# A hybrid block and two attention layers on one core: the first norm's sums folded on VectorE, the identity loaded by itself, modulation copies and one branch's masks put earlier

## What is computed

```python
def rmsnorm(x, g):
    y = xf * lax.rsqrt(jnp.mean(xf * xf, axis=-1, keepdims=True) + EPS)
    return (y * g).astype(x.dtype)

h = rmsnorm(x, norm1_g[l])                       # first norm
(hg_q, hg_f, hg_i, hg_g, ml_qk, ...) = jnp.split(h @ w_in[l], split_at, axis=-1)
# third branch, ssd_scan, per chunk (all chunks are taken as one here):
L = jnp.exp(jnp.where(tri, cum[..., :, None] - cum[..., None, :], NEG_BIG))
CB = jnp.repeat(jnp.einsum('btgn,bsgn->bgts', Cc, Bc), hpg, axis=1)
y_intra = jnp.einsum('bhts,bshp->bthp', CB * L, xdt)
# second block, per layer:
sh1, sc1, g1, sh2, sc2, g2 = modulation(c, w_ada[i], b_ada[i])
```

## Time and profile before

| | us |
|---|---|
| three runs | 1884.54, 1893.31, 1894.9 |
| their median | 1893.31 |
| the profiled execution, and its span | 1895.75, 1894.0 |
| PE busy | 1803.6 (95%) |
| DVE, ACT, POOL busy | 1014.4, 872.5, 358.4 |
| mean granted clock of PE | 0.962 of full speed |

### The profile page before, as it was taken

How to read it: one execution, slowest core, us unless ns; L and a number is a source line. 1 busy time by engine, 2 the same in 40 slices (tenths; PEclk the granted TensorE clock), 3 DMA queues, 4 the chain that set the end, 5 groups by cost and what they waited for, 6 DMA issues and landing times.

```text
span 1894.0 us, 30494 instructions
## 1 busy us (share of the span) xinstructions
PE 1803.6 (95%) x12882; PEld 1619.9 (86%) x12882; DVE 1014.4 (54%) x1760; ACT 872.5 (46%) x1261; POOL 358.4 (19%) x220
## 2 busy tenths in 40 slices
PE   7999989999999999999998999999999897889999
PEld 6999888888999999998866778877888786689999
DVE  1376469676766882465544165413552366438750
ACT  4422545547445664444653144312433345546653
POOL 4402540000000116500001301142114100041137
PEclk9999989999999999999986989999999898979999
DMA  6554445455455544511100332254223221025544
GB/s 253 208 193 167 168 189 189 156 201 200 193 221 212 190 167 138 178 68 46 46 1 1 134 112 89 75 188 171 98 83 121 95 90 67 1 90 180 183 151 155
DMA packets 40823, 258.78 MB, mean 137 GB/s; under 512 B 4336, under 2 KB 7408, under 8 KB 14320
## 3 DMA queue, kind: packets, MB, share of 16 engines
q1 hardware_dynamic: 40688, 256.84, 37.1%
HBM read 255.77 MB, written 1.05 MB: 136 GB/s over the span
## 4 chain that ended last, share of the span: by engine, by line
PE 83%; DVE 11%; ACT 3%; issue 1%; DMA 1%; POOL 1%; SPq 0%; DVEq 0%; ACTq 0%
PE acc_psum L194 22%; PE acc_psum L195 21%; PE acc_psum L196 21%; PE acc_psum L2213 4%; PE acc_psum L2173 2%; PE acc_psum L235 2%; DVE w_low_sb L160 2%; PE acc_psum L2195 2%; PE acc_psum L319 2%; PE acc_psum L911 2%; PE acc_psum L254 1%; DMA con_sb<-in_con 1%; DVE norm_sq_sb L570 1%; DVE norm_rt_sb L1561 1%; POOL w_low_sb L160 1%
## 5 line engine op out<-in xcount | busy, mean ns | idle before, releaser
L194 PE MATMUL acc_psum<-h_high_sb,w_high_sb 128*128 128x256 f32 (+1 forms) x2144 | 667.5, 311 | 9.1 <-DVE h_low_sb L379 4.4
L196 PE MATMUL acc_psum<-h_high_sb,w_low_sb 128*128 128x256 f32 (+1 forms) x2144 | 658.8, 307 | 0.0
L195 PE MATMUL acc_psum<-h_low_sb,w_high_sb 128*128 128x256 f32 (+1 forms) x2144 | 658.6, 307 | 0.0
L149 ACT ACTIVATE w_high_sb<-ring_sb 128x1024 fp32r<-128x1024 f32 (+2 forms) x412 | 386.6, 987 | 455.3 <-PE acc_psum L196 250.4
L194 PEld LDWEIGHTS acc_psum<-h_high_sb,w_high_sb 128*128 128x128 f32 x2144 | 411.8, 192 | 40.0 <-issue 16.8
L160 POOL TENSOR_TENSOR w_low_sb<-ring_sb,w_high_sb 128x1024 fp32r<-128x1024 f32 (+2 forms) x150 | 297.3, 2005 | 744.2 <-ACT w_high_sb L149 744.2
L195 PEld LDWEIGHTS acc_psum<-h_low_sb,w_high_sb 128*128 128x128 f32 x2144 | 411.5, 192 | 19.2 <-issue 0.5
L196 PEld LDWEIGHTS acc_psum<-h_high_sb,w_low_sb 128*128 128x128 f32 x2144 | 410.9, 192 | 18.4
L160 DVE TENSOR_TENSOR w_low_sb<-ring_sb,w_high_sb 128x1024 fp32r<-128x1024 f32 (+1 forms) x262 | 306.6, 1211 | 85.7 <-ACT w_high_sb L149 75.9
L1774 DVE SCALAR_TENSOR_TENSOR u_filtered<-acc_psum,par_sb,u_filtered 128x255 f32<-128x255 f32 (+2 forms) x264 | 150.8, 571 | 151.4 <-ACT u_filtered L1881 139.2
L1909 POOL TENSOR_TENSOR u_low<-u_filtered,u_high 128x256 fp32r<-128x256 f32 (+1 forms) x66 | 61.0, 924 | 785.0 <-ACT u_high L1902 785.0
(11 more groups left out here) (290 smaller groups left out, 2143.0 us busy)
## 6 DMA issues: line engine op xcount, KB each, us to landing
ring_sb<-in_w_in SPq DMA_DIRECT2D x68, 1024.0 KB, 6.4
ring_sb<-in_w_up SPq DMA_DIRECT2D x66, 1024.0 KB, 4.8
ring_sb<-in_w_ada SPq DMA_DIRECT2D x48, 1024.0 KB, 4.9
ring_sb<-in_w_down SPq DMA_DIRECT2D x48, 704.0 KB, 4.1
ring_sb<-in_w_out SPq DMA_DIRECT2D x12, 1024.0 KB, 5.1
ring_sb<-in_w_br_hg SPq DMA_DIRECT2D x4, 1024.0 KB, 7.4
ring_sb<-in_w_br_ml SPq DMA_DIRECT2D x4, 1024.0 KB, 7.8
ring_sb<-in_w_br_mb SPq DMA_DIRECT2D x4, 1024.0 KB, 8.4
```

Of the source, the lines that this page charges most:

```text
L149: self.nc.scalar.activation(self.high[:, g % 2, piece], self.ring[:, c % RING, piece], ACT.Copy)\
L194: nc.tensor.matmul(out, sh, mh, start=start, stop=False)
L195: nc.tensor.matmul(out, sh, ml, start=False, stop=False)
L196: return nc.tensor.matmul(out, sl, mh, start=False, stop=stop)
```

## The change

- The identity is loaded by a DMA of its own, right behind x; the later DMA of the constants takes the rest (`con[:, P:]`). PE waits for the identity alone ahead of the spread, and for the rest at unit 1.
- ACT first takes a Sqrt of two constants (into `norm1.tokens`, overwritten later), then squares, then makes the first unit's high part, then the root. Before, the high part stood behind the root.
- DVE adds the four tiles of squares in three operations of 512 columns and one of 256; PE sums the one folded tile with `folded_sums`, two products in place of 16.
- DVE waits for `par` behind the reciprocal, no longer ahead of it.
- In DVE's loop the modulation copy stands right behind the read-out of unit n - 1, ahead of the scan steps of the first branch and of the low part of unit n + 1.
- In iteration 45 `mb_keep_cb` stands ahead of the reciprocal and values of the second branch's norm.

```diff
--- before.py
+++ after.py
@@ -321,6 +321,15 @@
                                                stop=(k == len(self.streams) - 1 and t == DT - 1 and b == ST - 1), skip_group_check=True)
         if p == DT // 2 - 1:
             mm.then_inc(*self.summed.one())
+
+    def folded_sums(self, pe, folded):
+
+        core = self.core
+        pe.wait_ge(*folded.at(1))
+        for b in range(ST):
+            mm = core.nc.tensor.matmul(core.psum[:, self.bank, b:b + 1], self.streams[0].v(0)[:, b * P:(b + 1) * P], core.ones[:, 0:1],
+                                       start=(b == 0), stop=(b == ST - 1), skip_group_check=True)
+        mm.then_inc(*self.summed.one())
 
     def root(self, act, *biases):
 
@@ -710,6 +719,8 @@
                 for half in range(2):
                     sp.dma_start(X[:, 4 * half:4 * half + 4, 0:S], a["x"].rearrange("(k p) t -> p k t", p=P)[:, 4 * half:4 * half + 4, :])\
                         .then_inc(*x_ready[half].dma())
+                o_, w_ = CON_AT["ident"]
+                sp.dma_start(con[:, o_:o_ + w_], a["con"][:, o_:o_ + w_]).then_inc(*sig("identity_ready").dma())
                 core.load(sp, 0)
                 sp.dma_start(par[:, :], a["par"]).then_inc(*par_ready.dma())
 
@@ -841,6 +852,7 @@
         "parameters_ready", "constants_set", "constants_ready", "conditions_ready"))
     done, act_read, dve_read = sig("unit_done"), sig("unit_read_by_act"), sig("unit_read_by_dve")
     filtered, conv_read = sig("conv_filtered"), sig("conv_read")
+    folded, identity = sig("squares_folded"), sig("identity_ready")
     mk_ready, wg_ready, mk_kept = sig("level_masks_ready"), sig("gate_weights_ready"), sig("level_masks_kept")
     mixed_ready, mixed_high, mixed_low = sig("mixed_ready"), sig("mixed_high_ready"), sig("mixed_low_ready")
 
@@ -1272,7 +1284,7 @@
         def _(sp):
             for c in range(1, RING):
                 core.load(sp, c)
-            sp.dma_start(con[:, :], a["con"]).then_inc(*con_ready.dma())
+            sp.dma_start(con[:, P:], a["con"][:, P:]).then_inc(*con_ready.dma())
             sp.dma_start(lv_in, a["levels"]).then_inc(*mk_ready.dma())
             sp.dma_start(flat(wg), a["w_gates"]).then_inc(*wg_ready.dma())
             core.release(sp, UNITS, mods[0])
@@ -1340,12 +1352,14 @@
                     mods[r // NM].reduce(pe, r, r % NM)
 
             pe.wait_ge(*const_set.at(1))
-            for p in range(DT // 2):
-                norm1.sums(pe, p)
-
-            pe.wait_ge(con_ready.handle, 16)
+            norm1.folded_sums(pe, folded)
+
+            pe.wait_ge(identity.handle, 16)
             norm1.spread(pe)
             for n in range(UNITS):
+                if n == 1:
+
+                    pe.wait_ge(con_ready.handle, 16)
                 unit(n)
                 modulation(n)
                 for i in hg_steps(n):
@@ -1453,15 +1467,15 @@
                 s = 2 * (c % 2)
                 nc.scalar.activation(dst, conv_tmp[:, s:s + 2, :], ACT.Silu).then_inc(*conv_read.one())
 
+            act.wait_ge(*const_set.at(1))
+            nc.scalar.activation(norm1.tokens, core.eps[:, 0:2], ACT.Sqrt)
             for p in range(DT // 2):
                 if p % 2 == 0:
 
                     act.wait_ge(x_ready[p // 2].handle, 16)
                 norm1.square(act, p)
-
-            act.wait_ge(*const_set.at(1))
+            core.split_high(act, 0)
             norm1.root(act, core.eps[:, 0:1])
-            core.split_high(act, 0)
             norm1.highs(act)
 
             act.wait_ge(par_ready.handle, 16)
@@ -1594,8 +1608,16 @@
                 if b == 2:
                     dve.sem_inc(*mixed_ready.one())
 
+            sq = core.norm_sq
+            dve.wait_ge(*norm1.at(norm1.squared, 2))
+            link(nc.vector.tensor_tensor(sq[:, 0, :], sq[:, 0, :], sq[:, 1, :], ALU.add))
+            dve.wait_ge(*norm1.at(norm1.squared, 4))
+            link(nc.vector.tensor_tensor(sq[:, 2, :], sq[:, 2, :], sq[:, 3, :], ALU.add))
+            link(nc.vector.tensor_tensor(sq[:, 0, :], sq[:, 0, :], sq[:, 2, :], ALU.add))
+            nc.vector.tensor_tensor(sq[:, 0, 0:S], sq[:, 0, 0:S], sq[:, 0, S:2 * S], ALU.add).then_inc(*folded.one())
+            norm1.reciprocal(dve)
+
             dve.wait_ge(par_ready.handle, 16)
-            norm1.reciprocal(dve)
             norm1.parts(dve)
             for n in range(UNITS + 1):
                 if n == 1:
@@ -1604,6 +1626,9 @@
                     nc.vector.tensor_reduce(mods[0].select, cn("ident").rearrange("p (g s) -> p s g", g=4)[:, 0:2, :], AX.X, ALU.add)
                 if n >= 1:
                     evict(n - 1)
+                if n - 1 in rides:
+                    r = rides.index(n - 1)
+                    mods[r // NM].copy(dve, r)
                 steps = list(hg_steps(n - 1))
                 for i in steps[:1]:
                     hg_step(dve, i)
@@ -1611,9 +1636,6 @@
                     low(n + 1)
                 for i in steps[1:]:
                     hg_step(dve, i)
-                if n - 1 in rides:
-                    r = rides.index(n - 1)
-                    mods[r // NM].copy(dve, r)
                 if n == 2 * NM + 1:
                     mods[0].read(dve, NM, 0, NM).then_inc(*first_read.one())
                 if n == 4:
@@ -1638,6 +1660,8 @@
                     hg.value(dve, link, n - 32)
                 if 34 <= n < 38:
                     hg.part_low(dve, n - 34)
+                if n == 45:
+                    mb_keep_cb(dve)
                 if n in (42, 45):
                     ml.reciprocal(dve, link, 0 if n == 42 else 1)
                     for p in (0, 1) if n == 42 else (2, 3):
@@ -1646,8 +1670,6 @@
                     ml.part_low(dve, n - 45)
                 if n in (43, 44):
                     mb_keep_turned(dve, n - 43)
-                if n == 45:
-                    mb_keep_cb(dve)
                 if 47 <= n < 55:
                     mb_weights(dve, n - 47)
                 if 46 <= n < 54:
```

## The result

The changed kernel takes **1876.54 us** (median of 5 executions, 1872.22 to 1879.53). The kernel before, run beside it, had a median of 1887.1; the ratio is 0.9919 with a 95% interval of [0.9891, 0.9946]. So it is faster, by about 15 us if one goes by the ratio (the two medians of five differ by 10.6), where the sum of the prediction was 9.8. The profiled execution of the changed kernel took 1873.61 us for a span of 1871.8 us, at a mean granted clock of 0.970; that of before had 0.962.

What follows compares the result with a forecast made beforehand. TensorE was taken to set the end, with 83% of the chain of waits. Gains of 5.1 + 2.9 + 1.5 + 0.3 = 9.8 us took the median from 1893.31 to 1883.5 us, range 1876 to 1890.

Steps and rivals of the forecast that it cites:

- The head, 5.1 us: Kernel start: TensorE's first weight product at 15.05 instead of 20.17, 5.1 us earlier; bounds 4.6 and 6.0.
- The hold of VectorE's first low part by GpSimd: Head: VectorE's first low part, beside GpSimd's low parts, ends 0.3 us behind GpSimd, at 14.9.
- rival A: Head: no hold by GpSimd, TensorE starts at 14.2; sum 10.7, time 1882.6 us; chance 0.12.
- the landing of the tile: Head: identity's load ahead of the first weight tile costs 0.3 us, tile lands at 8.7; bounds 0 to 0.5 us.
- That whole chain moves by the same: Unit 1: its VectorE, ScalarE and GpSimd parts hang on the first low part and move by the same 5.1 us.
- Rival D: Head's gain taken back by unit 2's load, late behind other loads; only 4.7 us remain, 1888.6 us; chance 0.07.
- The masks, 2.9 + 1.5 us: n = 45: TensorE's mask wait goes, 2.9 us, and the 1.2 GHz stretch behind it, 1.5 us.
- rival C: Mask wait only traded for a later wait with its half-clock stretch; sum 5.4, time 1887.9 us; chance 0.10.
- The copies, 0.3 us: Modulation copies moved ahead of scan steps and low parts: 0.3 us saved at the reduce at 503.61; bounds 0 to 0.5.
- the clock term of 1.5 us: Behind the mask wait, 415.1 to 418.5: without idling the clock stays at 2.4 GHz, 1.5 us gained; bounds 0 to 1.7.

Runs made afterwards that it cites:

- e4: The changed kernel measured again beside its three separate parts; median 1873.1 us, ratio 0.9921 to the kernel before.
- e11: The changed kernel with ScalarE's split of the first unit's high part put back behind the root; median 1875.3 us, ratio 0.9934 to the kernel before.
- e15: The kernel before with 50 unused products on TensorE at n = 28, in the wait behind the gate sums; median 1886.9 us, ratio 0.9992.
- e13: The kernel before with 25 unused products at n = 51, where TensorE never waits, shifting later work by 3.0 us; median 1890.4 us, ratio 1.001.
- e16: Repeat of the changed kernel with 50 unused products at n = 28, in the wait behind the gate sums; mean 1878.3 us.
- e2: The kernel before with only the masks' move in iteration 45; median 1879.2 us, ratio 0.9944.
- e9: The kernel before with 22 unused products on TensorE at n = 45, filling the wait for the masks; median 1882.9 us, ratio 0.9968.
- e10: The changed kernel with 50 unused products at n = 28, in the wait behind the gate sums; mean 1877.5 us, ratio 0.9943 to the kernel before.
- e14: The changed kernel with 25 unused products at n = 51, where TensorE never waits; median 1884.2 us, ratio 0.9958 to the kernel before.

## Why the prediction was right or wrong

**The head, 5.1 us: mechanism right, size 4.5.** The hold of VectorE's first low part by GpSimd was there as worked out (1.30 us, ending 0.27 behind GpSimd; rival A is out), the table load was hidden, and the sums and the spread left the path. The term that failed is the landing of the tile: 8.7 by its bytes and an issue slot, bounds 8.4 to 8.9, measured 9.8 in this profile and 9.2 to 9.8 over nine. I had priced 64 KB at 432 GB/s; it cost 0.7 to 1.35 us, in the mean 1.0, the rate of some 68 GB/s. (The head's own bound of 4.6 had allowed for a tile at 9.2, and 4.4 to 4.5 lies just below it.) The first product moved by 4.1 in this profile; by unit 2 the lead was 4.1 here and 4.6 in e4's profile. "That whole chain moves by the same" was right in kind, and e11 shows on what: VectorE's later low parts, not the first product. Rival D, a late load of unit 2, did not occur; TensorE's waits at 25.45 and 27.70 are GpSimd's, as in the earlier trace rows. Squares ran behind a Sqrt without a load of their own. The Trainium skill ("ScalarE: Activation LUTs", section "What ACT_TABLE_LOAD costs") makes its 2.7 us up of a load of about 1283 ns and a drain of about 1380 ns; the load's row here has the same 1.28 us, and no drain is seen on it, as the Sqrt of the changed kernel starts 0.01 us behind its end (2.03).

**The masks, 2.9 + 1.5 us: right at their place.** The wait went whole, the local stretch at 1.2 GHz with it, and nothing came in its place (rival C): the lead in the profiles grows by 7.7 - 4.7 = 3.0 us at the wait and by 1.5 behind it. The rule that I had weighed, that the place of the transition varies between executions (the Trainium skill, "TensorE: Matmul & The Clock Gate", Part 1), holds here for where the stretch begins (0.2 to 1.7 us behind the wait) and, in e15, for its length, but not for whether there is one: that goes with the idling (5 of 5 profiles with it, 0 of 13 without). At other places it does vary: between 720 and 820 us half-clock time is 10.2 us in the profiles of before, e13 and e16, 6.8 in those of e2, e9 and e10, and 0 to 3.4 in the rest.

**The copies, 0.3 us: borne out at its place, too small to see in the time.** The reduce of the earlier trace rows gained 0.4 us of lead; the mean shows nothing. (There are 34 copies, one for each odd unit, not 32; nothing in the sum hangs on it.)

**The sum at equal clock** was 5.1 + 2.9 + 0.3 = 8.3, with the local stretch 9.8. Measured is 7.9 +- 0.4 of work for the 8.3 (6.7 with the slope of 1.9), and 6.9 of clock for the 1.5 (8.1). That is where the forecast failed: **the clock term of 1.5 us was mis-sized**, 6.9 by the executions. I had asked only what the clock does next to the edit and taken all later stages as fixed. They are not: their half-clock stretches differ from execution to execution, and their mean differs between kernels. Of the 6.9, 1.5 are shown at the mask wait itself. Most of the rest comes with the same wait in the mean: the masks' move alone has a clock part of -4.7 and the mere filling of the wait (e9) one of -5.1, the head's edits -1.8. How an idling at 413 lowers the clock of later stages stays open. It may be that their mean goes with the times at which they start: shifts of 3 us with no idle time touched moved the clock part by 2 us one way (within its scatter) and 4.5 the other (e13, e14), and e10 and e16 lost again what they had gained at their place. So these 5 us belong to this kernel as timed, and a next edit that moves the stages by 3 us may take them, as e14 seems to.

**The level.** The forecast of 1883.5 went by the median of three, 1893.31. From the usual 1889.5 the same sum gives 1879.7; the rest to 1874.2, 5.5 us, is the clock term. Both errors, 4 us of the level and 5 of the clock, made the forecast too high, and 1876.54 lies at the low edge of the range. That the work came out so near, 7.9 for 8.3, doesn't confirm each of its terms: the head gave 0.6 less than forecast, and the masks by their work part 4.5 +- 0.8 for 2.9.

## What to carry to other kernels

Where one engine is busy 95% of the time and its clock has two levels, read the mean granted clock of every execution beside its time: at equal clock 8 us could be told to about 1 us here (0.4 of scatter, and the choice of the slope), from raw medians of a few executions hardly to 3. A single profile isn't a measure of tenths: the same tile landed anywhere from 9.2 to 9.8. Count a step only by what it hands on to the next dense stretch (here VectorE's later low parts), and look at which single instruction ends a wait: 34 copies were moved for 0.3 us, one moved past the filter ahead of it gave 4.3. A small load ahead of a large one that the path waits for is priced by what a run shows, not by its bytes.

## What I had not expected of the hardware

- A load of 64 KB in rows of 512 bytes (128 columns of f32 for each of 128 partitions), issued just ahead of a 1 MB tile, delayed the tile by 0.7 to 1.35 us, in the mean of nine profiles against two by 1.0, as much as some 410 KB at the 432 GB/s of the earlier trace rows.
- VectorE's subtraction of 128x256 beside GpSimd ended 0.27 to 0.28 us behind GpSimd's whole instruction, whichever of them was caught: 1.05, 1.30, 1.31 and 2.19 us in the place of 0.41. GpSimd's piece took about 5.9 us in the place of 2.35 where VectorE's fill of 3072 columns began 0.5 to 0.6 us behind it, and its usual 2.4 where the fill began 0.7 us or more behind (4 and 12 profiles).
- Waits of 2.1, 2.9 and 6.4 us of TensorE at these two places ended in, or were followed within 1.7 us by, a stretch at 1.2 GHz in every profile; filled with products of no use, they had none. In the mean over the executions the filling gave 5.7 us at the masks and nothing that can be told at the gate sums.
